# Expert gathers that leave empty places out, gate and up weights in 8 KB pieces, and h2 with permuted columns

## What is computed

```
h2 = rmsnorm(x) * (1 + scale2) + shift2                 # (1152, 1024)
lg = h2 @ w_group + b_group                             # 4 groups, take the best
le = h2 @ w_expert + b_expert                           # 32 experts, best two in the group
block b of 128 places belongs to one expert; slot_tok[place] = token, or none
yb = (silu(xb @ w_gate[e]) * (xb @ w_up[e])) @ w_down[e]   # xb: rows of h2 by slot_tok
x  = x + gate2 * (w1 * yb[dest1] + w2 * yb[dest2])
y  = rmsnorm(x) * final_g
```

## Time and profile before

| | |
|---|---|
| median of 3 runs | 1889.56 us (1889.5 to 1892.87) |
| the profiled execution: its time | 1889.39 us |
| the profiled execution: its span | 1887.7 us |
| PE / DVE / ACT / POOL busy | 91% / 50% / 40% / 14% |
| DMA, whole span | 371.36 MB, mean 197 GB/s |
| median runs against the profiled one | 0.17 us apart |

### The profile page before, as it was taken

The page is one execution under the profiler, slowest core; times in us unless marked ns, Lnnn a source line. Parts: engine busy times, 40 slices in busy tenths (PEclk is TensorE's granted clock), DMA queues, the critical chain, the costliest instruction groups (busy, mean ns, idle before and its releaser), DMA issues.

```text
span 1887.7 us, 22614 instructions
## 1 busy us (share of the span) xinstructions
PE 1708.9 (91%) x8539; PEld 1399.3 (74%) x8539; DVE 947.6 (50%) x1156; ACT 755.3 (40%) x869; POOL 261.1 (14%) x327
## 2 busy tenths in 40 slices
PE   6984999999989999999999997189999999999976
PEld 1244987887549989999999786177777777877753
DVE  0451101554321263222213544858888888888857
ACT  0221123664111112111112222157777777777753
POOL 2003501110000000000000000402121212212003
PEclk9996999999999999999999998589999999999988
DMA  9757622002512110121114433089999999999967
GB/s 343 279 99 204 207 73 73 1 1 92 160 68 79 36 45 27 51 83 52 47 51 136 181 124 134 15 330 397 400 396 400 397 399 398 398 399 397 400 223 276
DMA packets 194749, 371.36 MB, mean 197 GB/s; under 512 B 10700, under 2 KB 69108, under 8 KB 194547
## 3 DMA queue, kind: packets, MB, share of 16 engines
q1 hardware_dynamic: 170784, 289.92, 42.7%
q0 software_dynamic: 18976, 62.93, 10.4%
q10 hardware_dynamic: 4914, 17.49, 2.3%
HBM read 324.49 MB, written 47.89 MB: 197 GB/s over the span
## 4 chain that ended last, share of the span: by engine, by line
PE 72%; DMA 12%; DVE 8%; issue 3%; ACT 2%; another core or an unknown queue 2%; SPq 0%; POOL 0%; DVEq 0%; ACTq 0%; PEldq 0%; POOLq 0%
PE ps L1547 12%; PE ps L1548 12%; PE ps L1549 12%; DMA mraw<-in_w_e_down_dram 9%; PE ps L1530 4%; PE ps L1870 4%; PE ps L1871 4%; PE ps L1877 3%; PE ps L1674 3%; PE ps L1655 2%; PE ps L1897 2%; PE ps L1905 2%; PE ps L1898 2%; PE ps L1737 2%
## 5 line engine op out<-in xcount | busy, mean ns | idle before, releaser
L1064 DVE TENSOR_TENSOR mlo<-mraw,mhi 128x2048 fp32r<-128x2048 f32 x188 | 427.5, 2289 | 78.0 <-ACT mhi L931 77.8
L931 ACT CAST mhi<-mraw 128x2048 fp32r<-128x2048 f32 x192 | 366.6, 1913 | 111.5 <-DMA mraw<-in_w_e_down_dram 76.4
L1547 PE MATMUL ps<-hTh,ring_r 128*128 128x384 f32 x864 | 291.3, 337 | 38.3 <-DVE ring_r L1064 31.1
L1548 PE MATMUL ps<-hTl,ring_r 128*128 128x384 f32 x864 | 290.5, 336 | 0.0
L1549 PE MATMUL ps<-hTh,ring_r 128*128 128x384 f32 x864 | 290.2, 336 | 0.0
L1870 PE MATMUL ps<-mhi,xTh 128*128 128x512 f32 x512 | 204.6, 400 | 2.7 <-DVE xTl L1064 2.4
L1871 PE MATMUL ps<-mhi,xTl 128*128 128x512 f32 x512 | 201.5, 394 | 0.0
L1547 PEld LDWEIGHTS ps<-hTh,ring_r 128*128 128x128 f32 x864 | 163.5, 189 | 39.7 <-DVE ring_r L1064 29.3
L1064 DVE TENSOR_TENSOR ring_r<-ring_f,ring_r 128x1024 fp32r<-128x1024 f32 x56 | 68.3, 1224 | 197.8 <-ACT ring_r L741 197.4
L1548 PEld LDWEIGHTS ps<-hTl,ring_r 128*128 128x128 f32 x864 | 163.6, 189 | 0.0
L1549 PEld LDWEIGHTS ps<-hTh,ring_r 128*128 128x128 f32 x864 | 163.6, 189 | 0.0
(11 more groups left out here) (304 smaller groups left out, 2604.7 us busy)
## 6 DMA issues: line engine op xcount, KB each, us to landing
mraw<-in_w_e_gate_dram SPq DMA_DIRECT2D x64, 1024.0 KB
mraw<-in_w_e_up_dram SPq DMA_DIRECT2D x64, 1024.0 KB
mraw<-in_w_e_down_dram SPq DMA_DIRECT2D x64, 1024.0 KB, 12.6
aring<-in_w_ada_dram SPq DMA_DIRECT2D x24, 1024.0 KB
ring_f<-in_w_in_dram SPq DMA_DIRECT2D x80, 256.0 KB, 4.5
y_d<-yy ACTq DMA_DIRECT2D x32, 512.0 KB, 6.8
y_d<-zrow POOLq DMA_DIRECT2D x68, 128.0 KB, 4.1
kc<-in_cache_attn_k_dram SPq DMA_DIRECT2D x8, 1024.0 KB, 5.9
```

Source lines behind the costliest of these rows:

```text
L931: nc.scalar.copy(mhi[j][:], mraw[j][:]).then_inc(s["gu_hi" if j < 4 else "d_hi"], 1)
L1064: V.tensor_tensor(out, value, high.bitcast(F32), ALU.subtract).then_inc(sig, 1)
L1547: mm(out, xh, wh, start=start, stop=False)
L1548: mm(out, xh, wl, start=False, stop=False)
```

## The change

1. `gather` and the overflow gather take a bound: an index above 1151 is left out, that is, no row is read for it and that partition of `xg` keeps what it had. The token numbers in the table are counted from 1 (`tokid`); a place that holds 0 gets 65536 added, and 1 is taken off all, so that an empty place has an index outside the bound.
2. The gate and up weights are laid out by `(p k)` in place of `(k p)`: partition p holds rows 8p to 8p + 7, so that a half of 1 MB brings one piece of 8 KB to each partition. The down weights stay.
3. To match, column p * 8 + k of h2 stands at k * 128 + p: L1308 writes a buffer `h2n` and L1310 writes `h2` in the permuted order. `h2_d`, the gathered rows and their transposes follow, and so do the router's weights.

```diff
+EMPTY = 65536.0
...
+        h2n = at("h2n", [P, D], A(140.5))
...
-            gate_d = w_e_gate[0].rearrange("e (k p) n -> p e k n", p=P)
-            up_d = w_e_up[0].rearrange("e (k p) n -> p e k n", p=P)
+            gate_d = w_e_gate[0].rearrange("e (p k) n -> p e k n", p=P)
+            up_d = w_e_up[0].rearrange("e (p k) n -> p e k n", p=P)
             down_d = w_e_down[0].rearrange("e (k p) n -> p e k n", p=P)
...
-                return (w[:, ex, k0:k0 + kn] if isinstance(ex, int)
+                rows = (w[:, ex, k0:k0 + kn] if isinstance(ex, int)
                         else w[:, bass.ds(ex, 1), k0:k0 + kn].rearrange("p e k n -> p (e k) n"))
+                return rows.rearrange("p k n -> p (k n)") if j < 4 else rows
 
             def place_of(j):
-                return mraw[j][:].rearrange("p (k n) -> p k n", k=4 if j < 4 else 2)
+                return mraw[j][:] if j < 4 else mraw[j][:].rearrange("p (k n) -> p k n", k=2)
...
-            nc.gpsimd.iota(tokid[:], [[P, NT]], base=0, channel_multiplier=1,
+            nc.gpsimd.iota(tokid[:], [[P, NT]], base=1, channel_multiplier=1,
                            allow_small_or_imprecise_dtypes=True).then_inc(s["consts"], 1)
...
-                pool.dma_start(wr[:, :, 0:G], w_group[0].rearrange("(k p) g -> p k g", p=P)
+                pool.dma_start(wr[:, :, 0:G], w_group[0].rearrange("(p k) g -> p k g", p=P)
                                ).then_inc(s["wr_in"], 16)
-                pool.dma_start(wr[:, :, G:NLOG], w_expert[0].rearrange("(k p) g -> p k g", p=P)
+                pool.dma_start(wr[:, :, G:NLOG], w_expert[0].rearrange("(p k) g -> p k g", p=P)
                                ).then_inc(s["wr_in"], 16)
...
                 pool.indirect_dma_start(out=xg[:, r, :], out_offset=None, in_=h2_d,
-                                        in_offset=bass.IndirectOffsetOnAxis(ap=idx[:, r:r + 1], axis=0)
+                                        in_offset=bass.IndirectOffsetOnAxis(ap=idx[:, r:r + 1], axis=0),
+                                        bounds_check=T - 1, oob_is_err=False
                                         ).then_inc(s[f"xg_in{r}"], 16)
...
-                link(V.scalar_tensor_tensor(out=h2[:, r, :], in0=x1[:, t, :], scalar=sumsq[:, 1, t:t + 1],
+                link(V.scalar_tensor_tensor(out=h2n[:], in0=x1[:, t, :], scalar=sumsq[:, 1, t:t + 1],
                                             in1=scale2[:, side, :], op0=ALU.mult, op1=ALU.mult))
-                V.tensor_tensor(h2[:, r, :], h2[:, r, :], shift2[:, side, :], ALU.add).then_inc(s["n2_h"], 1)
+                V.tensor_tensor(h2[:, r, :].rearrange("t (k p) -> t p k", k=KT),
+                                h2n[:].rearrange("t (p k) -> t p k", k=KT),
+                                shift2[:, side, :].rearrange("t (p k) -> t p k", k=KT), ALU.add
+                                ).then_inc(s["n2_h"], 1)
...
-            V.tensor_copy(table[:], ps[:, 2, 0:NBLK]).then_inc(s["route_done"], 1)
+            link(V.tensor_scalar(blki[:], ps[:, 2, 0:NBLK], 0.0, EMPTY, ALU.is_equal, ALU.mult))
+            V.scalar_tensor_tensor(out=table[:], in0=ps[:, 2, 0:NBLK], scalar=-1.0, in1=blki[:],
+                                   op0=ALU.add, op1=ALU.add).then_inc(s["route_done"], 1)
```

More of the change, by code:

```diff
@@ L699, in _ @@
                         pool.indirect_dma_start(out=xg[:, 0, :], out_offset=None, in_=h2_d,
-                                                in_offset=bass.IndirectOffsetOnAxis(ap=idx[:, 0:1], axis=0)
+                                                in_offset=bass.IndirectOffsetOnAxis(ap=idx[:, 0:1], axis=0),
+                                                bounds_check=T - 1, oob_is_err=False
                                                 ).then_inc(s["o_xg"], 16)
```

## The result

| | before | after |
|---|---|---|
| median | 1889.56 us (1887.86 to 1892.87, 5 runs) | 1880.75 us (1878.99 to 1881.97, 5 runs) |
| ratio after / before | | 0.995, 95% interval 0.9935 to 0.9964 |
| profiled execution: time, span | 1889.39, 1887.7 us | 1881.97, 1879.6 us |
| experts' stage: one period (mean of 28) | 18.430 us | 18.007 us |

A forecast was written before the change was run, and what follows sets the result against it. DMA was taken to bound the experts' stage at 18.43 us per expert, with PE next at 17.81. Terms -17.4 + 0.25 + 0.4 - 0.3 = -17.1 us from 1889.39 gave 1872.3 us, range 1870 to 1881.5.

The forecast's parts named there:

- rival B: Experts' stage: the ACT, DVE, PE chain keeps half of the 0.62 us idle; period 18.1, time 1881; chance 0.12.
- PE's floor: Experts' stage: PE's own work per expert, taken as 17.81 us from one period without idle before L1918.
- What bounds the kernel: Experts' stage: DMA sets the 18.43 us period through late down halves; PE's own work is 17.81 us.
- Part 1: Expert gathers: leaving out 56 empty rows per expert saves 0.23 MB, 0.57 us at 398 GB/s.
- The first gather: -0.3: Path into the experts' stage: fewer rows shorten the first gather by 0.3 us, between 0.6 less and 1.3 more.
- Part 2: Gate and up weights: 8 KB pieces at 419 GB/s help make PE the bound at 17.81 us; stage 17.4 less.
- Part 3: Norm's permuted h2 write, L1310: tile 8 uncovered, +0.4 us between 0 and +1.2; tiles 0 to 7 hidden.
- Part 4: Table before the first gather: one more DVE instruction on 49 columns, +0.25 us on the path.
- A: Experts' stage: 8 KB pieces give nothing, only the gathers help; period 17.95, gain 13.4 us, 1876; chance 0.10.
- C: Experts' stage: skipped places cost like full ones, pieces cut as before; 1889.5 to 1890 us; chance 0.05.
- D: Gate and up reads 16 KB apart served slower; at 350 GB/s period 19.0, 16 us slower, 1906; chance 0.05.

The follow-up runs named there:

- the pieces alone: Changed kernel without the gathers' bounds (empty places gather token 0 again); 8 KB pieces and permuted h2 stay; ratio 0.9901, period 17.694 us.
- even places: Changed kernel with only ranks below 64 of each block placed, in the even places; ratio 0.9906, period 17.694 us.
- bit 5 clear: Changed kernel with only ranks below 64 placed, in places 0 to 31 and 64 to 95; ratio 0.9881, period 17.733 us.
- places 0 to 63: Changed kernel with only ranks below 64 of each block placed, in the lower 64 partitions; ratio 0.9946, period 18.059 us.
- bit 4 clear: Changed kernel with only ranks below 64 placed, in places 0 to 15, 32 to 47, 64 to 79, 96 to 111; ratio 0.9931, period 17.946 us.
- the spread kernel: Changed kernel with each block's tokens dealt to even places first and then to odd ones; ratio 0.991, period 17.694 us.

## Why the prediction was right and wrong

Faster was right, 1880.75 lies in the range of 1870.0 to 1881.5, but by its upper end: the forecast itself, 1872.3, was 8.5 us too low. It lands on rival B's 1881 and nearly on its period (18.1), for another reason than B gives.

Of the miss, 5.6 us lie in the stage (17.4 less were forecast, 11.8 measured), where two errors pull opposite ways: PE's floor lay lower than thought, worth 3.2 us more, and leaving rows out cost 8.8. Most of the rest lies in the head, which scatters. That the range held all the same is luck in part: its upper end stood at rival B's time, not at one for this mechanism.

**What bounds the kernel: right, with a floor 0.12 us too high.** The DMA set the period, through late down halves. But PE's own work per expert is 17.69 us, the same in four kernels, not 17.81. The lone period of 17.81 in the earlier trace rows, the next to last, had a little waiting in it: the same period takes 17.69 in the pieces alone. Half of the difference stands at its very start, behind the transpose that had waited for `hh`: 167 ns to the next start, and 110 in the pieces alone. The number was in view elsewhere. PE's weight loads waited 19.5 us for `hh` in the 27 periods of the earlier trace rows, 0.72 us each, and 18.43 - 0.72 = 17.71. Read again on the changed kernel: 8.3 + 1.0 us over 27.8 periods are 0.33, and 18.01 - 0.33 = 17.68. So 20.6 us were to be had in the stage, not 17.4.

**Part 1, the failed step.** It costed 56 rows less as "56 x 4 KB = 0.23 MB per expert go, 3.1% of 7.34 MB; at 398 GB/s 0.57 us", that is, as if bytes gone from any partition relieved the whole DMA. They relieve the engines of their own partitions. Alone the part brought 18.430 - 18.312 = 0.12 us a period, and on top of the pieces it cost 0.31. The sign on top of the pieces is the part that was not foreseen by any rival. The bound itself costs POOL nothing: its issue takes 2435 ns against 2528 over 1284 to 1782 us, and where the engines are evenly relieved 1.02 us against the 1.25 of the pieces alone. "The first gather: -0.3" came to nothing: from its issue to PE's start it is 4.65 us (below) against 4.68 in the earlier trace rows. Leaving every row out made PE's idle there 4.30 us in place of 6.44, and starts were 2.58 us after issue, so rows do count there. How much they count goes by engine here too: with 64 of the 128 rows, issue to start was 3.92 us (even places) and 3.86 (bit 5 clear), but 4.44 (places 0 to 63) and 4.66 (bit 4 clear).

```profile
1225.94 0.18 POOL L680 COPY idx<-table 128x1 int32<-128x1 int32 x1 [18.30 <-DVE table L1424]
1227.09 1.28 POOL L683 DMA_INDIRECT xg<-h_d,idx  x1 [0.97 <-POOL idx L680]
...
1231.74 0.45 PE L1871 MATMUL ps<-ident,xg 128*128 128x128 f32 x1 [6.44 <-DMA xg<-h_d,idx]
```

**Part 2, right, and worth more than forecast.** With PE's floor lower than thought, the pieces alone brought the 20.6 us. Longer runs per partition do move faster. 415 GB/s was the mean of the pieces alone, 419 the value taken for gate and up. Their packets give the prices, as medians of the records in the stage: 88 ns for 2 KB, 159 for 4 KB, 309 for 8 KB, that is 176, 159 and 154.5 ns for each 4 KB. Most of the gain lies in the step from 2 to 4 KB.

**Part 3, too low.** +0.4 was taken for tile 8 between 0 and +1.2. L1315 took 1.90 us there against 1.23 in the earlier trace rows, so +0.67, and PE's idle before the tile's transposes grew from 4.56 to 5.23 by the same 0.67:

```profile
1167.63 1.90 DVE L1315 TENSOR_TENSOR h<-h2n,shift 128x1024 f32<-128x1024 f32 x1
```

```profile
1169.59 0.69 PE L1840 MATMUL ps<-ident,h 128*128 128x128 f32 x2 [5.23 <-DVE h L1315]
```

The eight tiles before it took 2.01 to 2.03 us each, and the cover held but for tile 0, where PE waited 0.24 us for `h`; in the second profile of the changed kernel no such wait reaches 0.15. The rule of the Trainium skill (SBUF — State Buffer, Door 1: The DMA port swizzle) on 16-byte lines had the right sign; the trace puts its price, at a stride of 512 B, at a factor of 1.55 to 1.65 for this instruction, not at 2. Most of the 5.4 us by which the first rows came late is not seen to be the change's: the out projection's matmuls on `mixh` begin at 1054.0 us and not at 1049.5, behind stages whose code is the same but for the two reads of the router's weights, and from there to the table it is 0.9 us more than before. In the ten other profiled executions the first rows start anywhere from 1226.9 to 1231.2 us, so the head scatters by some us from run to run. That the two reads have no part in it is not shown. The stage's period does not (18.007 and 18.009 in two profiled executions of the changed kernel).

**Part 4, right.** 0.21 + 0.21 us on 49 columns in place of 0.21, one after the other with 0.24 us between the starts: +0.24 against +0.25.

```profile
1225.42 0.21 DVE L1423 TENSOR_SCALAR route<-ps 128x49 f32<-128x49 f32 x1 [1.98 <-PE ps L1862]
1225.66 0.21 DVE L1424 SCALAR_TENSOR_TENSOR table<-ps,route 128x49 int32<-128x49 f32 x1
```

**The rivals.** A said that the pieces give nothing: they gave all. B said that the chain of ACT, DVE and PE keeps some idle though the DMA has slack. The profile after looks just like its mark (share at 1.00, idle before L1928), and its 18.1 is near. But with the same chain and six single buffers the spread kernel, the one with even places and the pieces alone all ran at PE's floor, so the chain keeps nothing by itself; what it passes on is the lateness of the loaded engines. C fell with 8 KB packets and 0.56 MB in q0. D fell with 415 GB/s: a pitch of 16 KB between neighbouring partitions did not keep the core under what it moved before.

**What stays open.** The eight loaded engines have in the changed kernel nearly the same bytes as in the pieces alone, and yet a down half lands 2.7 us later. Relieving the others should at worst have done nothing. The records do not tell why. Between 1300 and 1770 us fewer than 16 packets are under way in 9.5% of the time, against 1.9% with the pieces alone, and a 4 KB packet takes 180 ns in the mean, against 165; but the even kernels that leave rows out show the same (7.4% to 9.0%, 177 to 193 ns) at PE's own pace, so neither is the cause. That the relieved engines start the next requests earlier and so change the order in which the loaded ones serve gathers, stores and weights is argued and not shown. What is shown is that unevenness over the engines is the condition (with 8 KB pieces, three uneven kernels in four profiles at 17.95 to 18.06, six even ones at 17.69 to 17.74).

## What to carry to other kernels

Count DMA work by engine, not by bytes: a transfer is as late as its last engine, and bytes taken from one half of the partitions can make a stage slower. If places are left out, spread those that stay over the groups of four partitions. And for the time a bound would leave, subtract the wait that ends on the critical engine from the period; one period that looks free may still have some of it inside.

## What the runs showed of the hardware beyond that

- A place left out by the bound still puts a packet of 4 bytes and 9 ns on the queue; with no row gathered at all q0's share is still 0.5%, and a gather still lands 5.0 us after its issue.
- The landing of a gather got quicker by the 8 KB pieces of the weights beside it (9.3 us before, 7.5 with the pieces alone). Leaving rows out on one side took that back (9.7 in the changed kernel), leaving them out evenly added to it (6.2 in the spread one).
- With 8 KB pieces this one core moved 415 GB/s as a mean over 470 us. Single slices of 0.9 us reached 446 in the view above, but a slice counts a packet's bytes where it starts.
- The same gather's issue on POOL takes 2.4 to 2.5 us in the stage wherever PE still waits for the DMA, 1.0 to 1.25 us in the kernels that run at PE's pace, and 1.28 us for the first gather, ahead of the stage. Why is not shown.
